# Softmax division of the sliding attention, on VectorE or on GpSimd

## The reference, cut to what matters

```python
def sink_attention(q, k, v, sinks, key_ok):
    s = jnp.einsum('bcqkgd,bcskd->bckgqs', q, k, ...) * (HEAD_DIM ** -0.5)
    s = jnp.where(key_ok[None, :, None, None, None, :], s, NEG)
    sink = jnp.broadcast_to(sinks..., s.shape[:-1] + (1,))
    p = jax.nn.softmax(jnp.concatenate([s, sink], axis=-1), axis=-1)[..., :-1]
    return jnp.einsum('bckgqs,bcskd->bcqkgd', p.astype(v.dtype), v)
```

## Time and profile before

| | |
|---|---|
| time, 3 runs | median 1887.36 us (1886.79 to 1889.73) |
| the profiled execution | 1884.98 us, span 1883.3 us |
| busy in the span | PE 1721.5, PEld 1100.3, DVE 857.6, ACT 750.2, POOL 550.0 us |
| granted TensorE clock, mean | 0.964 of full speed |
| `window_attention` | from about 1097 to 1245 us of the span |
| L1271, the four multiplications | 40.1 us busy, 144 instructions |

### The profile page before, as it was taken

The page is one execution under the profiler, slowest core; times in us unless marked ns, Lnnn a source line. Parts: engine busy times, 40 slices in busy tenths (PEclk is TensorE's granted clock), DMA queues, the critical chain, the costliest instruction groups (busy, mean ns, idle before and its releaser), DMA issues. The chain is left out here.

```text
span 1883.3 us, 25928 instructions
## 1 busy us (share of the span) xinstructions
PE 1721.5 (91%) x9822; PEld 1100.3 (58%) x9822; DVE 857.6 (46%) x1596; ACT 750.2 (40%) x1590; POOL 550.0 (29%) x436
## 2 busy tenths in 40 slices
PE   5989995599999999999999969979999999859996
PEld 5954442366666666666666635545555555547775
DVE  5724333022222222222232259968878787743332
ACT  4512444122222222222222136645556565646564
POOL 0002321212223222222223000015556565624443
PEclk8999998799999999999999979989999999979998
DMA  4310013111000010111110011210011000456662
GB/s 129 117 25 23 11 61 1 35 30 30 23 30 30 30 58 34 58 41 30 30 64 29 25 62 46 77 49 29 25 68 36 23 14 12 146 140 173 178 182 92
DMA packets 121319, 108.14 MB, mean 57 GB/s; under 512 B 34768, under 2 KB 96496, under 8 KB 121200
## 3 DMA queue, kind: packets, MB, share of 16 engines
q1 hardware_dynamic: 118048, 95.62, 18.0%
q0 software_dynamic: 3152, 10.91, 1.5%
HBM read 65.54 MB, written 41.08 MB: 57 GB/s over the span
## 5 line engine op out<-in xcount | busy, mean ns | idle before, releaser
L330 PE MATMUL side_acc<-hT,wslot 128*128 128x512 f32 (+1 forms) x1360 | 586.9, 543 | 1.5 <-DMA wslot<-in_w_in 1.5
L1578 POOL TENSOR_TENSOR beta<-beta,prod 128x512 f32<-128x512 f32 (+4 forms) x184 | 225.6, 1238 | 329.0 <-DVE prod L1596 230.4
L330 PEld LDWEIGHTS side_acc<-hT,wslot 128*128 128x128 f32 x1360 | 217.5, 192 | 125.7 <-issue 119.2
L1596 DVE TENSOR_TENSOR_SCAN prod<-keepb,prod 128x512 f32<-128x512 f32 (+4 forms) x184 | 236.8, 1312 | 61.0 <-ACT keepb L1529 58.2
L964 DVE TENSOR_TENSOR xt<-xt,b_kq 128x512 f32<-128x512 f32 x85 | 58.4, 687 | 303.5 <-PE b_kq L791 303.5
L724 POOL TENSOR_TENSOR atl<-at,cf 128x512 f32<-128x512 f32 x102 | 139.7, 1402 | 173.3 <-DVE at L944 173.3
L460 PE MATMUL acc<-hT,wslot 128*128 128x512 f32 (+1 forms) x480 | 182.1, 536 | 5.3 <-DMA wslot<-in_w_in 5.3
L891 ACT ACTIVATE xm<-b_kq 128x512 f32<-128x512 f32 x85 | 50.7, 597 | 238.0 <-PE b_kq L778 237.8
L460 PEld LDWEIGHTS acc<-hT,wslot 128*128 128x128 f32 x480 | 85.2, 193 | 99.4 <-issue 93.8
L1708 PE MATMUL b_y<-whi,mhi 128*128 128x512 f32 x272 | 108.3, 398 | 21.7 <-DVE mlo L1761 21.7
L729 POOL TENSOR_TENSOR osq<-oo,ors 128x256 f32<-128x256 f32 x17 | 10.4, 612 | 387.3 <-ACT ors L925 387.3
(11 more groups left out here) (195 smaller groups left out, 2644.5 us busy)
## 6 DMA issues: line engine op xcount, KB each, us to landing
uT_scratch<-side_stage SPq DMA_DIRECT2D x36, 256.0 KB, 2.0
hT<-mix_scratch SPq DMA_DIRECT2D x17, 512.0 KB, 6.7
hT<-sz_scratch SPq DMA_DIRECT2D x17, 512.0 KB, 8.0
sz_scratch<-side_stage SPq DMA_DIRECT2D x32, 256.0 KB, 2.0
reg<-in_x_prompt SPq DMA_DIRECT2D x15, 512.0 KB
wslot<-in_w_in SPq DMA_DIRECT2D x15, 512.0 KB, 3.8
xres<-in_x_prompt SPq DMA_DIRECT2D x15, 512.0 KB
out_y_prompt<-yy POOLq DMA_DIRECT2D x15, 512.0 KB, 6.3
```

Source lines behind the costliest of these rows:

```text
L330: last = pe.matmul(self.acc[:, n % 2, 0:width], wslot[:, t % 2, k, :], hT[:, k, c0:c0 + width], start=(k == 0), stop=(k == KT - 1))
L1578: pool.tensor_tensor(w, w, prod[0:R, rowno[s] % 2, k0 + 1:k0 + nk + 1], ALU.mult).then_inc(w_ready, 1)
L1596: dve.tensor_tensor_scan(prod[0:R, row % 2, k0:k0 + nk][:, ::-1], kv, kv, prod[0:R, row % 2, k0 + nk:k0 + nk + 1], ALU.mult, ALU.bypass).t ...
```

## The change

The four multiplications on VectorE (L1271) go. In their place GpSimd gets a queue of its own in this stage, with one multiplication for each unit over all four heads: `pr` (rows x 4 heads x keys) times `rd`, whose one value for each row and head is repeated over the keys. The sum and the reciprocal stay on VectorE. `turn` now waits for one count of `normed` for each unit instead of four. The reciprocal of unit n gets a new wait: GpSimd must have read `rd` of unit n-2, whose buffer it overwrites.

```diff
@@ PE, turn(n)
-                            pe.wait_ge(normed, AG * (n + 1))
+                            pe.wait_ge(normed, n + 1)
@@ new: GpSimd's queue of the stage
+                    @block.gpsimd
+                    def _(pool):
+                        for n, (m, a) in enumerate(units):
+                            R, K = rows_of(m), keys(m)
+                            pool.wait_ge(recip_ready, n + 1)
+                            x = pr[0:R, n % 2, :, 0:K]
+                            pool.tensor_tensor(x, x, rd[0:R, n % 2, :].unsqueeze(2).to_broadcast([R, AG, K]), ALU.mult).then_inc(normed, 1)
@@ DVE, norm(n)
                             dve.wait_ge(den_ready, n + 1)
+                            if n >= 2:
+                                dve.wait_ge(normed, n - 1)
                             dve.reciprocal(rd[0:R, n % 2, :], den[0:R, n % 2, :]).then_inc(recip_ready, 1)
-                            dve.wait_ge(recip_ready, n + 1)
-                            for g in range(AG):
-                                x = pr[0:R, n % 2, g, 0:K]
-                                dve.tensor_scalar(x, x, rd[0:R, n % 2, g:g + 1], None, ALU.mult).then_inc(normed, 1)
```

## The result

| | kernel before | changed kernel |
|---|---|---|
| median, 5 runs each | 1889.73 us (1886.79 to 1892.78) | 1897.12 us (1896.73 to 1900.15) |
| profiled span | 1883.3 us | 1895.1 us |
| ratio to before | | 1.0050, 95% interval 1.0036 to 1.0064 |
| the same, measured again | 1885.35 us | 1893.45 us; 1.0045, 1.0031 to 1.0060 |

The change makes the kernel slower by 0.45 to 0.5%, that is 8 to 9 us.

The account below looks back on a forecast made before the run. DVE's queue was taken as the bound, at 3.89 us a unit, with two chains of waits close behind. 8.6 us over 32 units plus 0.3 and 0.8 at the ends gave 9.7; 1887.4 + 9.7 = 1897 us, range 1890 to 1914.

Parts of the forecast that it names:

- Chain A: Loop from DVE's keep copy through reciprocal, product and PE's transposes to the next keep: 3.33 us before, 4.13 forecast after.
- chain B: From a turn's end through PE's values and scores and DVE's bias to a keep: 4.16 us, unchanged.
- The product takes 1.88 us: GpSimd's product over 1024 elements, from a line through L729 and L711, which also have a repeated operand: 1.88 us.
- rival 1: GpSimd's product costs as much as with two full tensors, 2.35 us: 25 us slower, 1912 us; chance 20%.
- A unit takes the larger, 4.16: Period of a unit in the stage: the longer chain, 4.16 us against 3.89, 8.6 us over 32 units.
- Rival 3: DVE's relief wins if the product is under 1.37 us: with 1.04, 5 us less, 1882 us; chance 5%.
- The relief of DVE is worth nothing: Removing 1.06 us of multiplications a unit from DVE, some 34 us in all, gains only while DVE stays the bound.
- The new wait of the reciprocal costs nothing: DVE's reciprocal waits for GpSimd's product of n-3, already finished because the earlier keep needed a later product: no cost.
- The ends cost 1.1 us: Stage's ends: some 0.3 us for the first two units, 0.4 us for each of the last two, 0.8 together.
- The clock stays: PE's clock was forecast to remain at 1.00 in the changed stage.
- rival 5: PE pauses about 0.5 us each unit and its clock halves: stage over 64 us longer, 1960 us; chance 2%.
- DVE and GpSimd miss each other: DVE's operations with two SBUF inputs fall outside GpSimd's product, missing it by 0.9 us: nothing added.

Follow-up runs that it names:

- mid_values_dve: Kernel before, products still on DVE, with DVE's reciprocal moved before the keep copy and PE's values moved before turn: ratio 1.0004.
- mid_values_first: Changed kernel with DVE's reciprocal moved before the keep copy and PE's values moved before turn: 1871.95 us, ratio 0.9929.
- full_operand: Changed kernel with GpSimd multiplying by a full tensor of ones instead of the repeated reciprocal, probabilities left undivided: ratio 1.0117.
- values_first: Changed kernel with PE's step ordered scores, values, turn instead of scores, turn, values: ratio 1.0048.
- half_product: Changed kernel with GpSimd multiplying only two of four heads (512 elements), the others left undivided: ratio 0.9960.
- norm_first: Changed kernel with DVE's sum and reciprocal moved in front of the bias step and the keep copy: ratio 1.0111.
- split_heads: Changed kernel with two heads multiplied on GpSimd and two on DVE, PE's turn waiting for both: ratio 1.0081.

## Why the prediction was right

The forecast was 1897 us, 9.7 us over the kernel before; measured were 1897.12 us and 7.4 us between the medians, 9.4 by the ratio. That the absolute time agrees to 0.1 us is luck, since the medians of the kernel before moved by 2.4 us between the two sets of runs. The profiles give the stage 10.4 us, against 9.7 forecast; the sum came near because its small errors partly cancel. The steps:

- *DVE's queue is the bound, and two chains stand close behind it.* Right. In the kernel before, A and B take 3.33 + 4.16 = 7.49 of the 7.78 us of two units, so the loop had 0.29 us to spare. With the orders that cut the chains but DVE's products in place nothing changes (mid_values_dve, 1.0004); with DVE freed and the chains cut the stage falls to PE's own work (mid_values_first, 0.9929).
- *The product takes 1.88 us.* It took 1.894. The line through two shapes with a repeated operand was the right reading, and two full tensors (2.35, rival 1) the wrong one for this form: full_operand shows both numbers in one place. L724, which rival 1 had on its side, fits too: its operand is repeated over a middle axis, and its median for 512 elements is 1.267 us, as long as the product of two full tensors of that size in full_operand (1.261); L711, repeated along the inner axis, takes 1.03. The Trainium skill (GPSIMD Engine Reference, section 3.1) has the two inputs share one read port, which gave the estimate of 2.2 to 2.3 us. The traces agree for the full operand (2.34) and not for the repeated one (1.89).
- *Chain A 4.13, chain B 4.16 us.* Both right: values_first shows A alone (4.13), half_product that B is there (3.72 and not 3.5). *A unit takes the larger, 4.16:* not quite. The two alternate, and the prediction's own formula for rival 3 gives (4.16 + 2.25 + 1.88) / 2 = 4.145 us, which is what the steps of 4.13 and 4.16 show. That makes 8.2 us out of the forecast's 8.6. Measured were 9.0 over 31 periods, because of the one step of 4.52 and because the kernel before has shorter steps at the stage's two ends (3.60 and 3.59 at the start, 3.77 at the end), which the 3.89 left out. DVE waits for the scores each unit, but for the transposes only once in 24 units (0.3 us). I had expected to see both.
- *The relief of DVE is worth nothing.* Right in this order: 6.3 of its 20 us became idle time. The waits took its place one for one.
- *The new wait of the reciprocal costs nothing.* No such wait appears.
- *The ends cost 1.1 us.* Near in sum, 1.4, and wrong in both parts. The start was forecast to cost 0.3 us and gained 0.5: between the reciprocals of units 1 and 2 the changed kernel takes 2.73 us (1113.18 to 1115.91) instead of 3.21 (1112.96 to 1116.17), since DVE no longer has the short products in front of its next reduction. (PE's clock was also up earlier there, 1.00 instead of 0.50 between 1111 and 1112 us; the two are not told apart.) The end was forecast to cost 0.8 us and cost 1.9. From the last reciprocal with 256 keys to the transposes behind it, it takes 2.21 us instead of 1.41, so the last full product costs 0.8, where the forecast's thirty-second unit had counted 0.27. Each of the two short products costs 0.36, near the 0.4 forecast. The last 0.4 us come behind the last product, with the clock.
- *The clock stays.* Right in the middle of the stage, 1.00, and wrong at its end. In the kernel before, the granted clock is 1.00 until PE's last instruction of the stage. In the changed kernel PE does nothing between 1252 and 1253 us, where it waits for the last product, and from 1254.4 on the clock is 0.50. PE's last instruction, before and after, and the clock's row:

```profile
1244.35 0.44 PE L1208 MATMUL b_pt<-cf,reg 128*128 128x128 f32 x2
```

```profile
1254.74 0.69 PE L1208 MATMUL b_pt<-cf,reg 128*128 128x128 f32 x2
```

```profile
1254.50:1256.00 1.50, 0.93 (x6) 0.40 (x6) 0.72 (x2) 0.00 (x0) 0.00 (x0) 0.50 0.00 0
```

So what rival 5 feared happened, but only to PE's last few instructions of the stage, and cost about 0.4 us. In the second profile of the changed kernel the clock is down from 1251 us on, in front of its last transposes. It is not a matter of this change alone: mid_values_dve, with its products on DVE, also ends the stage with 0.69 us for this instruction.

- *DVE and GpSimd miss each other.* Right for the 32 long units, wrong for the last two, where the reduction is over 640 elements and `nm` starts earlier. The rows of DVE and then of GpSimd in the changed kernel:

```profile
1242.39 0.40 DVE L1263 SCALAR_TENSOR_TENSOR nm<-mx,nsink 32x4 f32<-32x4 f32 x1
```

```profile
1240.89 1.89 POOL L1245 TENSOR_TENSOR pr<-pr,rd 128x1024 f32<-128x1024 f32 x1 [2.25 <-DVE rd L1277]
```

`nm` ends at 1242.79, the product at 1242.78. It lasts 0.25 us too long and costs no time there: DVE then waits 0.99 us for the transposes, and the exponentials start behind ACT's keep at 1243.96. norm_first shows what the same meeting costs where it is on the path of each unit: 0.68 us, more than twice what the change itself costs.

Rival 3 (DVE's relief wins) had its condition right: a product under 1.37 us, or a shorter chain B together with a cut of A. half_product fulfils the first and is faster; its time was 7.5 us below the kernel before where the formula gave 5. The profiles have 4.9 us of it in the 31 periods (114.97 us instead of 119.88); where the rest lies was not looked for.

## What to carry to other kernels

A full engine is the bound only down to the next chain. Before moving work off it, follow one item through all the queues and add up every loop that comes back to the same instruction, with what stands in front of it in each queue: here the loop of two units had 0.29 us to spare, and the longer latency on the slower engine (chain A 4.13 us instead of 3.33) took 0.80, so that two units lost 0.51 us and one 0.26. The same move paid 13 us once the reciprocal no longer stood behind the copy and the scores no longer behind the values. Where two chains close only together, over two units, the period is half their sum and not the longer one. When GpSimd and VectorE both work on SBUF, look at the length of short VectorE operations, not at waits: a hold is recorded as busy time.

## What the runs showed of the hardware

- GpSimd's product of 128x1024 float32 takes 1894 ns when the second operand is one value repeated along the inner axis, and 2344 ns when it is a full tensor. A value repeated over a middle axis saves nothing at 128x512: median 1267 ns (L724 of the kernel before), against 1261 for a full tensor and 1038 for a value repeated along the inner axis.
- A DVE operation with two SBUF inputs that starts inside a GpSimd product ends with it: 0.84 instead of 0.16 us on four elements (norm_first), also 0.40 instead of 0.15 (the changed kernel's end). A reduction out of PSUM isn't held (1.19 us).
- DVE's float32 product with a scalar, SBUF to SBUF, is held as well, and is the one that loses: GpSimd's 1.04 us stayed, two of DVE's took 1.50 instead of 0.61 us (split_heads), and the first of them ended 0.15 us behind GpSimd's product. The Trainium skill (SBUF — State Buffer, on the shared port pair) gives the pair to the one that starts first. In the trace DVE's record starts 0.04 us earlier and GpSimd still isn't delayed; whether DVE really took the port first is not to be seen in it, so this stays open.
- TensorE's granted clock is 1.00 up to 1254.4 us and 0.50 behind it, at the end of the changed kernel's stage, after PE had stood idle from 1252 to 1253 us for a product; two transposes took 0.69 us there instead of 0.44.
